# Out-projection and experts in one program, index copies on ScalarE, outputs scaled in PSUM

## What is computed

```python
y = hs * gelu(gate_br)                      # the recurrent mixer's result
x = x + g1 * (y @ w_out)                    # out-projection, residual
h = rmsnorm(x, norm2_g) * (1 + sc2) + sh2
probs = softmax(h @ router_w + router_b)    # 16 experts in 4 groups of 4
# best group by the sum of its two largest; the two largest in it, gates normed to sum 1
x = x + g2 * sum_e gate_e * ((silu(h @ w_gate[e]) * (h @ w_up[e])) @ w_down[e])   # 256 wide
return rmsnorm(x, final_norm_g)
```

## Time and profile before

| what | value |
|---|---|
| median of 3 runs | 1388.54 us (1386.13 to 1388.87) |
| the profiled execution | 1389.41 us, its span 1387.8 us |
| busy share of the span | PE 79%, PEld 63%, DVE 61%, ACT 42%, POOL 51% |
| mean granted TensorE clock | 0.923 |
| moved by DMA | 232.62 MB, mean 168 GB/s |

### The profile page before, as it was taken

How to read it: one execution, slowest core, us unless ns; L and a number is a source line. 1 busy time by engine, 2 the same in 40 slices (tenths; PEclk the granted TensorE clock), 3 DMA queues, 4 the chain that set the end, 5 groups by cost and what they waited for, 6 DMA issues and landing times. The chain is left out here.

```text
span 1387.8 us, 21239 instructions
## 1 busy us (share of the span) xinstructions
PE 1093.6 (79%) x4860; PEld 878.0 (63%) x4861; DVE 848.6 (61%) x1217; ACT 582.2 (42%) x812; POOL 708.6 (51%) x752
## 2 busy tenths in 40 slices
PE   1359999999999992899999408487668778888881
PEld 0247778778778772788888406366556666666661
DVE  6994666766866845367776763355465655565653
ACT  1455667657667654122222103233343443343421
POOL 0555633633633600226676842156666666666653
PEclk9999999999999996999999658799898999999995
DMA  8446334335334125514545374366567667667642
GB/s 301 154 91 205 97 105 154 118 103 165 110 107 154 46 91 197 214 62 173 199 176 198 151 242 124 101 221 226 193 216 242 211 215 231 226 205 232 218 141 91
DMA packets 146301, 232.62 MB, mean 168 GB/s; under 512 B 34240, under 2 KB 101824, under 8 KB 145616
## 3 DMA queue, kind: packets, MB, share of 16 engines
q1 hardware_dynamic: 111248, 128.20, 28.5%
q0 software_dynamic: 23632, 62.49, 12.5%
q10 hardware_dynamic: 11376, 41.42, 9.2%
HBM read 177.45 MB, written 91.31 MB: 194 GB/s over the span
## 5 line engine op out<-in xcount | busy, mean ns | idle before, releaser
L1594 PE MATMUL e_gu<-w_hi,e_xh 128*128 x312 | 134.4, 431 | 37.0 <-DVE e_xl L1494 21.7
L1412 ACT ACTIVATE w_hi<-w_raw 128x1536 f32 x60 | 88.4, 1486 | 160.2 <-DMA w_raw<-in_moe_w_down_dram 96.8
L1275 POOL TENSOR_TENSOR w_lo<-w_raw,w_hi 128x1536 f32 x30 | 106.7, 3556 | 76.0 <-ACT w_hi L1412 39.0
L1596 PE MATMUL e_gu<-w_hi,e_xl 128*128 x312 | 127.7, 409 | 0.0
L1595 PE MATMUL e_gu<-w_lo,e_xh 128*128 x312 | 127.6, 409 | 0.0
L1157 PE MATMUL po<-wo_hi,b_yh 128*128 128x512 f32 x256 | 104.6, 408 | 27.8 <-DVE wo_lo L983 27.8
L1523 DVE SCALAR_TENSOR_TENSOR e_ob<-e_ab,e_rstd,e_fg 128x1024 f32<-128x1024 f32 x39 | 50.1, 1284 | 115.9 <-POOL e_rstd L1324 113.1
L543 DVE SCALAR_TENSOR_TENSOR XB<-xu,conv_w,XB 128x512 f32<-128x512 f32 x96 | 92.1, 960 | 42.3 <-ACT XB L413 38.7
L1617 PE MATMUL e_pd<-w_hi,e_ah 128*128 x156 | 71.3, 457 | 52.2 <-DVE e_al L1499 33.7
L636 PE MATMUL px<-hT_hi,wx_hi 128*128 128x512 f32 x256 | 101.7, 397 | 5.1 <-DVE wx_lo L477 5.1
L636 PE MATMUL pg<-hT_hi,wg_hi 128*128 128x512 f32 x256 | 104.3, 408 | 0.0
(11 more groups left out here) (272 smaller groups left out, 2862.4 us busy)
## 6 DMA issues: line engine op xcount, KB each, us to landing
e_xg<-hn_slots ACTq DMA_DIRECT2D x40, 512.0 KB, 4.9
e_xa<-x_slots ACTq DMA_DIRECT2D x39, 512.0 KB, 3.9
stg<-in_ada_w_dram POOLq DMA_DIRECT2D x32, 512.0 KB, 4.2
w_raw<-in_moe_w_gate_dram SPq DMA_DIRECT2D x32, 384.0 KB, 4.3
w_raw<-in_moe_w_up_dram SPq DMA_DIRECT2D x32, 384.0 KB, 5.0
n_ada<-in_ada_w_dram SPq DMA_DIRECT2D x16, 512.0 KB, 5.1
n_x<-in_x_dram SPq DMA_DIRECT2D x16, 512.0 KB, 3.3
hn_slots<-in_x_dram SPq DMA_DIRECT2D x16, 512.0 KB, 5.0
```

Source lines behind the costliest of these rows:

```text
L1275: tensor_tensor(w["lo"][:, ds(off + q * QW, QW)], w["raw"][:, q % 2], w["hi"][:, ds(off + q * QW, QW)].bitcast(F32), ALU.subtract).then_in ...
L1412: nc.scalar.activation(w["hi"][:, ds(off + q * QW, QW)], w["raw"][:, q % 2], ACT.Copy).then_inc(w["hi_done"], 1)
L1594: nc.tensor.matmul(gu[:], xh[:, tok], hi, start=(k == 0), stop=False)
L1596: last = nc.tensor.matmul(gu[:], xl[:, tok], hi, start=False, stop=(k == KD - 1))
```

## The change

Both programs become one, with no barrier between them. Waits of their own take its place: on the sends (`all_sent`), on the last two residual scatters (`sent_x`), on the tables (`tabled`). The expert stage's tiles lie over those of the out-projection; block 0's loads and gate_up use the constant slot 0 and expert 0. At the end of routing, tiles 13 and 14 are routed earlier, the last two tiles are sent in another order, and DVE adds the last tile's shift. Weights have four raw buffers; quarters 2 and 3 of expert 0 are read into the low part's second half. All 48 record loads stand in SyncE's queue ahead of expert 2's weights, and the first five of them free block 0. The scaled output stays in PSUM, `accumulate` and `normed` read one operand there, and `down` waits for `acc_ready` instead of `y_ready`. Both index copies move to ScalarE (`index_acc`, `index_out`) with the waits for the scatter before. The epsilon is added by a further column of the squared tile, and the root has four steps. `normed` and `accumulate` come a block earlier in DVE's order. The diff, its core:

```diff
-def load_quarter(sp, io, w, i, q):
-    raw, arrived = w["raw"][:, q % 2, :], w["in"][q]
+def load_quarter(sp, io, w, raws, i, q):
+    raw, arrived = raws[q][:], w["in"][q]
...
+                load_quarter(sp, io, w, w["raw"], 0, q)
+            sp.wait_ge(mm, NT)
             for q in range(2, NQ):
+                load_quarter(sp, io, w, w["raw"], 0, q)
+            for q in range(2):
                 sp.wait_ge(w["lo_done"][q % 2], 1)
-                load_quarter(sp, io, w, 0, q)
-            for q in range(2):
-                sp.wait_ge(w["lo_done"][q % 2], 2)
-                load_quarter(sp, io, w, 1, q)
-        @block.scalar
-        def _(act):
+                load_quarter(sp, io, w, w["raw"], 1, q)
...
+                if s == NT:
+                    act.wait_ge(mm, NT)
+                    high_w(0)
+                    high_w(1)
...
+            gate(NT - 1)
+            low_w(0)
+            low_w(1)
             logits(NT - 1)
             softmax_in(g)
+            choose(g)
             scale(NT - 1)
-            choose(g)
+            dve.wait_ge(scaled, NT)
+            v.tensor_tensor(hn[:, (NT - 1) % RING], hn[:, (NT - 1) % RING], sh2[:], ALU.add).then_inc(last_shifted, 1)
             assign(g)
...
+                if s >= NT - 2:
+                    send(2 * s - NT - 3)
+                    send(2 * s - NT - 2)
             root(NT - 1)
-            send(NT - 4)
-            shift(NT - 1)
-            for it in range(NT - 3, NT):
-                send(it)
-            q = 2
-            pool.wait_ge(w["hi_done"], q + 1)
-            wcols = slice(q * QW, (q + 1) * QW)
-            nc.gpsimd.tensor_tensor(w["lo"][:, wcols], w["raw"][:, q % 2], w["hi"][:, wcols].bitcast(F32),
-                                    ALU.subtract).then_inc(w["lo_done"][q % 2], 1)
-            for r in range(RING):
-                pool.wait_ge(sent[r], 160)
-        @block.tensor
-        def _(pe):
+            send(NT - 4 + 1)
+            pool.wait_ge(placed, NT // 2)
+            pool.wait_ge(last_shifted, 1)
+            for it in (NT - 2, NT - 1):
+                send_h(it)
+            for it in (NT - 2, NT - 1):
+                send_rec(it)
+            for it in (NT - 2, NT - 1):
+                send_x2(it, sent_x)
...
+            sp.wait_ge(w["sent"][0], 160)
             sp.dma_start(fg[:], io["final_norm_g"].partition_broadcast(P)).then_inc(fg_in, 16)
+            for r in (1, 2):
+                sp.wait_ge(w["sent"][r], 160)
             for q in range(2, NQ):
-                sp.wait_ge(w["lo_done"][q % 2], 3)
-                load_quarter(sp, io, w, 1, q)
-            for b in range(E, MAXB):
+                sp.wait_ge(w["hi_done"], q + 1)
+                load_quarter(sp, io, w, raw1, 1, q)
+            all_sent(sp)
+            sp.wait_ge(w["tabled"], 1)
+            for b in range(MAXB):
                 load_rec(b)
             for e in range(2, E):
                 for q in range(NQ):
-                    sp.wait_ge(w["lo_done"][q % 2], 2 * e + q // 2)
-                    load_quarter(sp, io, w, e, q)
+                    sp.wait_ge(w["lo_done"][q % 2], 2 * e - 1 + q // 2)
+                    load_quarter(sp, io, w, raw1, e, q)
...
-            def scatter_acc(b, first=False):
-                if not first:
-                    pool.wait_ge(acc_out, b * 16)
-                pool.nop(nofuse=True)
-                nc.gpsimd.tensor_copy(idx_a[:], recs[:, ds(b, 1), 0]).then_inc(idx_a_ready, 1)
+            def scatter_acc(b):
                 pool.wait_ge(idx_a_ready, b + 1)
                 pool.wait_ge(acc_ready, b + 1)
                 pool.nop(nofuse=True)
-                pool.indirect_dma_start(dr["x2"], rows(idx_a), ab[:], None, bounds_check=SLOTS - 1, oob_is_err=False)\
+                pool.indirect_dma_start(dr["x2"], rows(idx_a), ab, None, bounds_check=SLOTS - 1, oob_is_err=False)\
                     .then_inc(acc_out, 16)
-            def scatter_out(b, first=False):
-                if not first:
-                    pool.wait_ge(out_done, b * 16)
-                pool.nop(nofuse=True)
-                nc.gpsimd.tensor_copy(idx_o[:], recs[:, ds(b, 1), 1]).then_inc(idx_o_ready, 1)
+            def scatter_out(b):
                 pool.wait_ge(idx_o_ready, b + 1)
                 pool.wait_ge(out_ready, b + 1)
                 pool.nop(nofuse=True)
...
             def root(b, first=False):
                 pool.wait_ge(squared, b + 1)
-                pool.nop(nofuse=True)
-                nc.gpsimd.tensor_scalar(var[:], ssq[:], EPS, 0.0, ALU.add, ALU.add).then_inc(rstd_step, 1)
-                pool.wait_ge(rstd_step, 4 * b + 1)
-                pool.nop(nofuse=True)
-                nc.gpsimd.tensor_tensor(root0[:], var[:], nhalf[:], ALU.pow).then_inc(rstd_step, 1)
-                pool.wait_ge(rstd_step, 4 * b + 2)
-                nc.gpsimd.tensor_tensor(part[:], root0[:], root0[:], ALU.mult).then_inc(rstd_step, 1)
-                pool.wait_ge(rstd_step, 4 * b + 3)
-                pool.nop(nofuse=True)
-                nc.gpsimd.tensor_scalar(part[:], part[:], var[:], -0.5, ALU.mult, ALU.mult).then_inc(rstd_step, 1)
-                pool.wait_ge(rstd_step, 4 * b + 4)
                 if not first:
                     pool.wait_ge(out_ready, b)
                 pool.nop(nofuse=True)
-                nc.gpsimd.tensor_scalar(rstd[:], part[:], 1.5, root0[:], ALU.add, ALU.mult).then_inc(rstd_ready, 1)
-            nc.gpsimd.memset(nhalf[:], -0.5).then_inc(halved, 1)
-            low_w(pool, nc.gpsimd.tensor_tensor, 0, 1)
-            low_w(pool, nc.gpsimd.tensor_tensor, 1, 1)
-            pool.wait_ge(halved, 1)
-            pool.wait_ge(rec_in[0], 16 * E)
-            scatter_acc(0, True)
-            low_w(pool, nc.gpsimd.tensor_tensor, 2, 1)
+                nc.gpsimd.tensor_tensor(root0[:], ssq[:], nhalf[:], ALU.pow).then_inc(rstd_step, 1)
+                pool.wait_ge(rstd_step, 3 * b + 1)
+                pool.nop(nofuse=True)
+                nc.gpsimd.tensor_scalar(part[:], root0[:], ssq[:], root0[:], ALU.mult, ALU.mult).then_inc(rstd_step, 1)
+                pool.wait_ge(rstd_step, 3 * b + 2)
+                pool.nop(nofuse=True)
+                nc.gpsimd.tensor_scalar(part[:], part[:], -0.5, 1.5, ALU.mult, ALU.add).then_inc(rstd_step, 1)
+                pool.wait_ge(rstd_step, 3 * b + 3)
+                nc.gpsimd.tensor_tensor(rstd[:], root0[:], part[:], ALU.mult).then_inc(rstd_ready, 1)
...
+            with pool.Fori(2, nless) as i:
+                low(i + 2)
+                scatter_out(i)
+                scatter_acc(i + 1)
+                root(i + 1)
...
+            def index_acc(b, first=False):
+                if not first:
+                    act.wait_ge(acc_out, b * 16)
+                act.nop(nofuse=True)
+                nc.scalar.activation(idx_a[:], recs[:, ds(b, 1), 0], ACT.Copy).then_inc(idx_a_ready, 1)
+            def index_out(b, first=False):
+                if not first:
+                    act.wait_ge(out_done, b * 16)
+                act.nop(nofuse=True)
+                nc.scalar.activation(idx_o[:], recs[:, ds(b, 1), 1], ACT.Copy).then_inc(idx_o_ready, 1)
...
+            all_sent(act)
             load_h(0)
+            act.wait_ge(w["sent_x"], 32)
             load_x(0)
+            act.wait_ge(fg_in, 16)
+            nc.scalar.activation(fgp[:], fg[:], ACT.Copy).then_inc(fg_ready, 1)
+            act.wait_ge(w["tabled"], 1)
+            nless = blocks_less(act)
...
+            act.wait_ge(rec_in[0], 16 * EARLY)
+            index_acc(0, True)
+            index_out(0, True)
...
+            for b in range(LEAD):
+                square(b, b == 0)
+                if b > 0:
+                    index_out(b)
+                load_x(b + 1)
+                high_a(b + 1)
+                tanh(b + 2)
+                high_x(b + 3)
+                index_acc(b + 1)
+                high_w(b + 2)
...
+            with act.Fori(LEAD, nless) as i:
+                square(i)
+                index_out(i)
+                load_x(i + 1)
                 high_a(i + 1)
                 tanh(i + 2)
                 high_x(i + 3)
+                index_acc(i + 1)
                 high_w(i + 2)
...
-            def y_scaled(b, first=False):
+            def y_scaled(b):
                 dve.wait_ge(d_mm, b + 1)
-                if not first:
-                    dve.wait_ge(acc_ready, b)
-                nc.vector.tensor_tensor(ysb[:], pd[:], g2row[:], ALU.mult).then_inc(y_ready, 1)
+                nc.vector.tensor_tensor(pd[:], pd[:], g2row[:], ALU.mult).then_inc(y_ready, 1)
             def accumulate(b, first=False):
                 dve.wait_ge(y_ready, b + 1)
...
                     dve.wait_ge(squared, b)
                     dve.wait_ge(out_ready, b)
                     dve.wait_ge(acc_out, b * 16)
-                nc.vector.tensor_tensor(ab[:], ysb[:], xa[:], ALU.add).then_inc(acc_ready, 1)
```

(52 more changed lines are left out.)

318 lines of the change are left out of this document (168 added, 150 removed).

## The result

The changed kernel takes 1548.51 us (median of 4 runs, 1545.03 to 1551.24), the kernel before 1387.34 us in the same comparison (1383.94 to 1388.87): a ratio of 1.116, interval 1.113 to 1.120. It is 11.6% slower, on the side that was forecast, and 35 us above the forecast of 1513. Its profiled execution took 1548.04 us for a span of 1546.4.

The account below looks back on a forecast made before the run. GpSimd's queue was taken to bound the kernel before, a ring through ScalarE and GpSimd the changed one. 888 + 28 x 18.1 + 7 x 12.5 + tail 30 gave span 1512, time 1513 us, forecast range 1465 to 1570.

Parts of the forecast that it names:

- The ring: ScalarE's conversion, GpSimd's low, output scatter, its landing, ScalarE's index copy, next conversion: 18.1 us per block with a conversion.
- the seam: Routing into expert stage without barrier: tables at 824 us, block 3's conversion ends at 888, 12 us earlier.
- Its terms: Parts of one ring turn: 0.25, 3.5, 0.5, 5.0, 1.0 and 7.9 or 7.75 us, making 18.15 or 18.0.
- L: Start of the output scatter to its landing, taken as 5.0 us.
- The count: From block 3 to block 38: 28 steps with a conversion at 18.1 us, 7 without at 12.5.
- The sum: 888 + 507 + 87 + a tail of 30 us: span 1512, time 1513 us.
- Steps without a conversion: Blocks without GpSimd's weight conversion: 7.5 us from landing to next scatter, plus 5.0 to its landing, 12.5 us each.
- Edits that cost nothing: PSUM scaling, down's later wait and raw buffers add nothing; PSUM writing 0.2 us less to 1.2 more, under VectorE's idle time.
- The premise: GpSimd's own queue sets the pace; moving both index copies off it would win 84 us were it still the pace.
- The faster rival: Expert stage: the ring is not closed in time and GpSimd stays the pace, 1287 us; chance 0.09.
- Short landing: Rival: output scatters land in 3.3 us, as in the quiet tail, giving 1453 us; chance 0.18.
- Long landing: Rival: output scatters take 8 us or more to land, giving 1618 us; chance 0.15.

Follow-up runs that it names:

- experiment 2: Changed kernel with ScalarE's two index copies moved behind its weight conversion high_w: 1380.49 us, ratio 0.992 to 0.998 to the kernel before.
- experiment 3: Changed kernel with GpSimd's two scatters ahead of its conversion: 1371.00 us, ratio 0.987 to 0.994 to the kernel before.
- experiment 7: Changed kernel with all low-part weight conversions on VectorE, none on GpSimd: 1348.14 us, ratio 0.971 to 0.978 to the kernel before.
- experiment 1: Changed kernel with both index copies and their waits back on GpSimd: 1415.44 us, ratio 1.019 to 1.027 to the kernel before.
- experiment 11: Kernel before with only its index copies moved to ScalarE, GpSimd keeping scatters ahead of conversion: 1371.81 us, ratio 0.987 to 0.992.
- experiment 6: Changed kernel with scaled output and norming's gain back in SBUF and down waiting for the scaling: 1559.52 us, ratio 1.122 to 1.134.
- experiment 10: Kernel before with all low-part weight conversions on VectorE, none on GpSimd: 1346.98 us, ratio 0.970 to 0.974.
- experiment 12: Changed kernel with ScalarE's copies behind its conversion, all low parts on VectorE, two weight quarters loaded after 20 records: 1327.78 us, ratio 0.954 to 0.960.
- experiment 4: Changed kernel with ScalarE's index copies behind its conversion and GpSimd's scatters ahead of its conversion: 1363.12 us, ratio 0.982 to 0.987.
- experiment 9: Changed kernel with index copies back on GpSimd and all low-part conversions on VectorE: 1332.07 us, ratio 0.959 to 0.965.
- experiment 5: Changed kernel with two unused 128x1024 copies added on ScalarE right behind the output index copy: 1564.69 us, ratio 1.127 to 1.136.

## Why the prediction was right, and where it was short

**The ring: right.** The signs of the ring that I named were there: the copy of the output index waits for "DMA out_dram" (223.5 us, 26 times), scatters 19.9 us apart, GpSimd's conversion released by ScalarE's, no waits for weights on ScalarE behind block 3, the clock under 0.93. The copy waited in 26 steps, though, not in some 35, and the two times named, tables at 824 and block 3's conversion at 888, were not met (the seam, below). Experiments 2, 3 and 7 each open the ring at another place, and each time it is gone; 1 takes the wait off ScalarE, and 11 shows the same wait without a ring.

**Its terms.** Over the 26 turns from 895 to 1500 us, forecast against measured means:

| term | forecast | measured |
|---|---|---|
| high_w's end to low's start | 0.25 | 0.25 |
| low on GpSimd | 3.5 | 4.16 (3.44 to 5.05, once 9.51 for two parts) |
| to the scatter | 0.5 | 0.18 |
| L, scatter to index copy | 5.0 | 5.85 (4.43 to 7.38) |
| to high_a | 1.0 | 1.55 (median 1.46) |
| to high_w's end, second block of an expert | 7.75 | 7.88 |
| the same, first block | 7.9 | 9.05 (8.60 to 9.65, 7 turns) |

The largest miss is in two terms that I took from rows in which the engines did not meet. In the ring ScalarE's conversion releases GpSimd and VectorE at nearly the same moment, and they hold each other up (rows below): 0.66 us on low (0.13 of them for the second part of the one double turn) and more than half of the 0.85 on L. The first block's term was short because I gave the slow clock 1.0 us between 0 and 2.9, and down ran slowly nearly to its end, 1079.07 to 1084.2 instead of the 2.9 us of a fast one. The granted clock is 0.50 from 1079 to 1083.5 us, the lower of its two levels, and 1.00 from 1084 to 1088; ahead of it TensorE had rested 4.73 us:

```profile
1079.07 0.79 PE L1647 MATMUL po<-w_hi,e_ah 128*128 x1 [4.73 <-DVE e_al L1531]
1079.66 0.63 PE L1648 MATMUL po<-w_lo,e_ah 128*128 x1
...
1083.50 0.50 PE L1648 MATMUL po<-w_lo,e_ah 128*128 x1
```

**The count.** I counted 28 steps with a conversion and 7 without. The scatters show 26 and 9 from block 3 to block 38: of the 28 conversions one belongs to block 3 itself, and one block holds two. That was 2 x (18.1 - 12.5) = 11 us too much, and hid part of the short ring.

**The sum.** Start of the scatter behind block 3's conversion, 884.10 against 892.25: -8.2. Steps with a conversion, 26 x 19.73 = 512.9 for 26 x 18.1: +42.4. The count: -11.2. Steps without, 9 x 13.1 for 9 x 12.5: +5.4. From there to the end 31.6 for 25.8: +5.8. Together +34 us on a span of 1512. The steps and the tail were short by 54 us, and 19 us of errors the other way, in the seam and the count, hid a third of that: so much of the closeness is luck.

**Steps without a conversion.** 14.0 in the loop where I had 12.5, 9 to 12.6 in the tail. The mean held, the pattern didn't.

**The seam: direction right, size off.** Block 3's conversion on ScalarE ends at 880.26, forecast 888 (the terms that I gave add up to 887), before 899.9. SyncE in the changed kernel:

```profile
815.30 55.05 SPq L1272 DMA_DIRECT2D e_recs<-rec_scratch  x48
870.39 0.43 SPq L702 DMA_DIRECT2D w_raw<-in_moe_w_gate_dram  x1
```

The 48 record loads take the 55 us forecast. The tables came at 813.7, not 824: the last root of routing is 4.0 us later than before (787.6 for 783.6) where I had 7.6, and from there to the tables pass 26.1 us instead of 35.3, 9.2 less where I had 2.4 less (1.2 - 3.6). Of the difference 3.9 us are one row of the kernel before, which I had passed over:

```profile
813.60 4.09 DVE L1054 TENSOR_TENSOR t_split<-d_second,d_flag 128x48 int32<-128x48 f32 x1
```

The same step takes 0.21 us in the changed kernel (812.30), where no conversion of GpSimd runs beside it; before, one did (814.19, 3.43 us). Which edit of the last tile gave the rest was not run.

**Edits that cost nothing: wrong in sign, small.** The PSUM operands gained some 10 us (experiment 6). My bracket had a small gain inside it, but for the write, not for the neighbour.

**The premise: half right.** I read GpSimd's own queue as the pace of the kernel before and priced its relief in full, 84 us for the copies. Taking 98 us off GpSimd gave that kernel 40 us (experiment 10), and taking the copies off it 15 (experiment 11). The faster rival's 1287 stood on that price, and the fastest arrangement with the ring open (experiment 12) takes 1328.

**What I had not seen.** The merged program with the copies on GpSimd as before is still 2.3% slower than the kernel before (experiment 1). The cause is read from wait rows, not isolated: GpSimd's new order puts the scatter behind the conversion, and VectorE waits for its landing. It fits that turning the order back brings 17 us (experiment 4 against 2), and that without GpSimd's conversion the merged program is the faster one (experiment 9 against 10). No run has the old order with the copies on GpSimd.

**Rivals.** Short landing (L 3.3) is refuted: no L under 4.43 in 26. The figure of 3.2 us that the Trainium skill gives for this transfer ("DMA: Bandwidth & Descriptors", Anatomy of one DMA) is below every one of them; the trace does not agree where weights travel beside it. In the six steps of the loop without a conversion the copy came 3.16 to 4.30 us behind the scatter's start and did not wait, so those scatters had landed by then. Long landing holds for none of the means, but its direction was half of the miss. The faster rival needed L + 13.1 under 13.7.

## What the runs showed of the hardware

**Two subtractions from SBUF on VectorE and GpSimd do not run beside each other.** VectorE in the changed kernel, to be read beside GpSimd's rows above:

```profile
1067.75 3.83 DVE L1303 TENSOR_TENSOR w_lo<-w_raw,w_hi 128x1536 f32 x1 [0.74 <-issue]
...
1087.57 1.76 DVE L1303 TENSOR_TENSOR w_lo<-w_raw,w_hi 128x1536 f32 x1 [0.54 <-ACT w_hi L1427]
```

Where GpSimd began first (1066.50, 3.47 us, to 1069.97), VectorE's ended at 1071.58, which is 1.61 us, about its own length, after that. Where VectorE began first, by 0.02 us (1087.57, 1.76 us), GpSimd's took 5.05: 1.58 us more than 3.47. The second waits until the first is through. In all 26 turns it is so: in 17 GpSimd began first and took 3.44 to 3.52 us, in the other 9 VectorE did and GpSimd took 4.54 to 5.05, or 9.51 for two parts. By this the trace agrees with the Trainium skill ("SBUF — State Buffer", Who interferes with whom), which tells of one pair of ports that such an instruction holds to its end. The earlier trace rows do not show it, but other rows of the kernel before did, at 813.60 above and here:

```profile
861.07 1.76 DVE L1275 TENSOR_TENSOR w_lo<-w_raw,w_hi 128x1536 f32 x1 [1.83 <-issue]
861.55 4.64 POOL L1275 TENSOR_TENSOR w_lo<-w_raw,w_hi 128x1536 f32 x1 [8.10 <-ACT w_hi L1412]
...
1053.62 1.76 DVE L1275 TENSOR_TENSOR w_lo<-w_raw,w_hi 128x1536 f32 x1 [0.53 <-issue]
1053.82 2.41 POOL L1293 DMA_INDIRECT x_slots<-e_ab,e_idx_a  x1 [0.87 <-POOL e_idx_a L1289]
```

**A scatter's issue on GpSimd is held up by it as well.** Of the 37 output scatters from 895 us on, 17 took 2.40 us and 20 took 1.09. All 17 started inside a conversion on VectorE, none of the 20 did: the one at 1070.14 ends at 1072.55, 0.97 us after VectorE's, and the 17 all end 0.96 to 0.98 us after it. In the kernel before 12 accumulate scatters took 2.40 to 2.42 us in the same way, like the one at 1053.82; 13 that started within 0.02 us of the start of VectorE's conversion took 0.97 or 0.98. The landing at 1070.14 is seen 6.42 us after the start, that of 1051.25 after 5.66; the means are 6.14 for the 17 and 5.31 for the 9 others of the ring. A turn of the ring pays in one place or the other, never in both: 1.57 us on low where VectorE begins first, 1.31 on the scatter's issue where GpSimd does.

**Between the index copy and high_a ScalarE has a gap of 1.25 us, under which 2.0 us of copies hid for the most part** (experiment 5). The rows show a load's issue in it (1057.91, 0.34 us); that the rest is register reads for the load's address is the code's order, no row lists them.

## What to carry to other kernels

A small instruction is priced by what it waits for and by what stands behind it in its queue. Before moving it, follow the wait through every engine until it comes back: here a 0.2 us copy closed a ring of 20 us, and moving either the copy or GpSimd's conversion by a few places opened it. Durations of rows in which two engines did not meet hold only as long as they don't; an order that releases both at once needs its own price. And relieve an engine by giving away its longest instruction (3.5 us on GpSimd, 1.8 on VectorE) before its shortest ones: that one edit took both kernels to some 3% under the kernel before.
